# Two-layer hybrid decoder: sums of squares per head by a product with a block matrix of ones, and inverse roots as an exponential of a logarithm

## The chip, the core and the metric

The kernel runs on one core of a Trainium2 chip. A core has five engines with queues of their own: TensorE (PE in the profile; its weight loads stand apart as PEld), VectorE (DVE), ScalarE (ACT), GpSimd (POOL) and SyncE (SP), which here issues most of the DMAs. They wait for one another through semaphores. The metric is the device time of one execution in microseconds (us), taken as the median over runs.

## What is computed

Two layers of a decoder over a prompt of 1024 tokens and a sample group of 8 x 4 = 32 tokens, side by side, so that 1056 columns go through every dense step. Each layer makes all queries, keys and values in one projection, normalises queries and keys per head, rotates a quarter of each head, runs two attention mixers, and ends in an output projection and a gated feed-forward block. The part that the change touches is this one:

```python
def rms_norm(x, g):
    xf = x.astype(jnp.float32)
    y = xf * lax.rsqrt(jnp.mean(xf * xf, axis=-1, keepdims=True) + EPS)
    return (y * g.astype(jnp.float32)).astype(x.dtype)

def mix_inputs(x, g_attn, w_in, qn_a, kn_a, qn_b, kn_b, pos):
    h = rms_norm(x, g_attn)
    proj = jnp.einsum('nld,de->nle', h, w_in)
    qa, ka, va, qb, kb, vb = jnp.split(proj, SPLITS, axis=-1)
    qa = rope_partial(rms_norm(heads(qa, N_HEADS_A), qn_a), pos)
    ka = rope_partial(rms_norm(heads(ka, N_HEADS_A), kn_a), pos)
    qb = rope_partial(rms_norm(heads(qb, N_HEADS_B), qn_b), pos)
    kb = rope_partial(rms_norm(heads(kb, N_KV_B), kn_b), pos)
```

A head has 64 channels; the norm needs, for each token and head, one over the root of the mean of 64 squares.

## The kernel before

Activations lie with channels on the 128 partitions and tokens along the free dimension (1056 = 3 pieces of W = 352). One unit of the projection stage gives 128 channels, that is two heads, for all tokens. A layer has 18 units: unit 0 (keys of the second mixer), unit 1 (its values), and then for each of four pairs p the units u = 2 + 4p (keys), u + 1 (queries of the first mixer), u + 2 (queries of the second) and u + 3 (values of the first mixer, or of the next pair). `project(u, slot, bank, ns)` makes the pieces `ns` of a unit in PSUM banks `bank`, `bank + 1`, `bank + 2`; a piece is 24 products of 352 columns (8 chunks, each as high x high, low x high and high x low parts, line 404), a whole unit 72. Units alternate between banks 0 to 2 and 3 to 5; banks 6 and 7 are for turns.

Of the 18 units of a layer 13 are queries or keys and are normalised (26 in the two layers). For each of them:
- ACT squares the 1056 columns out of PSUM into `t_buf[1]` (`head_squares`, L704; L734 for unit 0).
- DVE multiplies the projection by the gain into `t_buf[0]` (`roped`, L983), shuffles it into `t_buf[2]` (L987), and multiplies by cosines (L989), later by sines (L997), and adds (L999).
- PE sums the squares (`sum_heads`, L1348): nine products, each with 128 (at last 32) tokens of the squares as the stationary operand and the two columns of `blocks` as the moving one. The sums stand with tokens on partitions, in the first 18 columns of the unit's first bank.
- DVE makes means and reciprocals on these few columns (L992, L996, tile `head_means`); ACT takes roots and spreads each over 64 columns (`roots_of_heads`, L711).
- PE turns them back with nine transposes (`spread_heads`, L1358), so that the inverse roots stand on all channels in the unit's three banks, and DVE multiplies (`k_rope` L1005 into `kt_all`, `q_rope` L1010 and L1014 into `xm` and the sample rows, with a factor of -1).

PE's order is written out by hand: `sum_heads` of a unit comes after the first piece of the next unit, `spread_heads` after its second. Between them stand the turns of keys and values (`turn`, L1366 and L1369: nine transposes each), which ACT (`keep_k`, L726 and L729) and DVE (`keep_v`, L1023 and L1026) take out. The values are turned from `stage`, which ACT fills (`stage_v`, L719) once the store of the keys that lay there has left (`k_out`). POOL splits the weights of each unit into high and low parts (L590, L593), beginning when the unit two before has been projected; SP loads them (`w_load`) and stores turned keys (`k_store`) and values in one order. The attention of the layer begins when every unit has been projected and rotated; then come output projection and feed-forward block, most of the layer.

## Time and profile before

| | us |
|---|---|
| median of three runs | 3083.45 (3083.42 to 3084.25) |
| the profiled execution, its own time | 3081.73 |
| its span, first to last instruction | 3080.1 |
| PE busy | 2887.1 (94%) |
| weight loads busy | 2666.2 (87%) |
| DVE busy | 1189.6 (39%) |
| ACT busy | 825.4 (27%) |
| POOL busy | 507.9 (16%) |
| projection stage of the first layer | 78.3 to 325.2 |

Times inside the profile are counted from the first instruction of the span. In a row of the timeline or of the groups, "out<-in" names the tiles by the program's names, then the shapes follow and "x18" is how many records the row merges. PE records overlap, since a product begins before the one ahead has left the array: the start to start distance is the cost of one, the duration isn't. In brackets stands how long the engine was idle before the instruction, and what it waited for. DMA issues stand under the queue of the engine that issues them (SPq, ACTq).

### The profile page before, as it was taken

Reading aid. Unit: us, or ns where it says so; the run is one execution under the profiler, and the core shown is the slowest. Engines: PE = TensorE matmul, PEld = TensorE weight load, DVE = VectorE, ACT = ScalarE, POOL = GpSimd, SP = SyncE. Lnnn points to the kernel's source line nnn. Section 1 sums busy time; section 2 is a strip of 40 time slices with the busy share of each in tenths; the row PEclk is TensorE's granted clock in tenths of the full one; section 3 lists DMA queues with packets and bytes.
Section 4 is the critical chain, followed back from the end, with each engine's and each line's share of the span. In section 5 each row is a group of like instructions: output and inputs, shape, how many; then the busy total and the mean of one; then the engine's idle time right before and its main releaser. Section 6 shows DMA issues by size and latency. Waiting matters only on the chain.

```text
span 3080.1 us, 52475 instructions
## 1 busy us (share of the span) xinstructions
PE 2887.1 (94%) x19546; PEld 2666.2 (87%) x19546; DVE 1189.6 (39%) x2524; ACT 825.4 (27%) x1612; POOL 507.9 (16%) x211
## 2 busy tenths in 40 slices
PE   4999999969899999999969999997889999999998
PEld 4999666569899999999959996665879999999998
DVE  5444555442422222223254445554442222223223
ACT  2111556531211121111031126565221111111110
POOL 1222000012211121112022210000221211122110
PEclk6999999979899999999989999998889999999999
DMA  4121453121455545411021224431245454444111
GB/s 157 43 62 49 117 150 101 51 91 62 166 187 184 179 152 178 151 41 45 9 93 49 55 60 142 128 99 40 91 139 171 152 178 151 151 158 158 41 41 56
DMA packets 182635, 333.36 MB, mean 108 GB/s; under 512 B 30481, under 2 KB 142097, under 8 KB 179665
## 3 DMA queue, kind: packets, MB, share of 16 engines
q1 hardware_dynamic: 171632, 195.20, 20.2%
q0 software_dynamic: 2816, 135.99, 13.3%
q8 instruction: 91, 1.49, 0.2%
q10 hardware_dynamic: 8032, 0.17, 0.2%
q14 instruction: 64, 0.52, 0.1%
HBM read 309.08 MB, written 157.94 MB: 152 GB/s over the span
## 4 chain that ended last, share of the span: by engine, by line
PE 90%; DVE 4%; issue 2%; ACT 2%; DMA 1%; DVEq 0%; ACTq 0%; SPq 0%
PE ps L404 68%; PE ps L1438 4%; PE ps L1452 3%; PE ps L1427 3%; PE ps L1348 2%; PE ps L1501 1%; PE ps L1358 1%; PE ps L1489 1%; PE ps L1470 1%; DVE g_lo L960 1%; DVE t_buf L945 1%; PE ps L1313 1%; DVE hf L945 1%; PE ps L1477 1%; DMA kt_all<-in_x_prompt_dram 1%
## 5 line engine op out<-in xcount | busy, mean ns | idle before, releaser
L404 PE MATMUL ps<-g_hi,f_hi 128*128 128x352 f32 x2496 | 815.6, 327 | 32.7 <-DVE g_lo L960 32.7
L404 PE MATMUL ps<-g_hi,f_lo 128*128 128x352 f32 x2496 | 811.3, 325 | 0.0
L404 PE MATMUL ps<-g_lo,f_hi 128*128 128x352 f32 x2496 | 810.0, 325 | 0.0
L404 PEld LDWEIGHTS ps<-g_hi,f_hi 128*128 128x128 f32 x2496 | 475.1, 190 | 38.2 <-DVE g_lo L960 38.2
L629 POOL TENSOR_TENSOR f_lo<-f_raw,f_hi 128x2048 fp32r<-128x2048 f32 x66 | 303.9, 4618 | 1195.8 <-ACT f_hi L877 1195.8
L404 PEld LDWEIGHTS ps<-g_hi,f_lo 128*128 128x128 f32 x2496 | 475.9, 191 | 0.0
L404 PEld LDWEIGHTS ps<-g_lo,f_hi 128*128 128x128 f32 x2496 | 475.6, 191 | 0.0
L1271 DVE TENSOR_TENSOR silu<-silu,ps 128x352 f32<-128x352 f32 x132 | 68.8, 521 | 820.0 <-ACT silu L899 820.0
L1281 DVE TENSOR_TENSOR xm<-xm,ps 128x352 f32<-128x352 f32 x528 | 271.0, 520 | 199.6 <-PE ps L404 199.6
L404 PE MATMUL ps<-a_hi,f_hi 128*128 128x352 f32 x1056 | 340.6, 323 | 0.0
L404 PE MATMUL ps<-a_hi,f_lo 128*128 128x352 f32 x1056 | 338.4, 320 | 0.0
L404 PE MATMUL ps<-a_lo,f_hi 128*128 128x352 f32 x1056 | 338.2, 320 | 0.0
L404 PE MATMUL ps<-h_hi,w_hi 128*128 128x352 f32 x864 | 288.5, 334 | 14.6 <-DVE h_lo L960 14.6
L404 PE MATMUL ps<-h_lo,w_hi 128*128 128x352 f32 x864 | 279.7, 324 | 0.0
L404 PE MATMUL ps<-h_hi,w_lo 128*128 128x352 f32 x864 | 278.9, 323 | 0.0
L899 ACT ACTIVATE silu<-ps 128x352 f32<-128x352 f32 x132 | 61.3, 465 | 653.4 <-PE ps L404 653.2
L404 PEld LDWEIGHTS ps<-a_hi,f_lo 128*128 128x128 f32 x1056 | 198.4, 188 | 0.0
L404 PEld LDWEIGHTS ps<-a_hi,f_hi 128*128 128x128 f32 x1056 | 198.1, 188 | 0.0
L404 PEld LDWEIGHTS ps<-a_lo,f_hi 128*128 128x128 f32 x1056 | 197.9, 187 | 0.0
L765 ACT ACTIVATE pt<-ps 128x512 f32<-128x512 f32 (+3 forms) x320 | 133.8, 438 | 218.0 <-PE ps L1438 217.3
L404 PEld LDWEIGHTS ps<-h_hi,w_hi 128*128 128x128 f32 x864 | 163.4, 189 | 19.1 <-DVE h_lo L960 17.4
L404 PEld LDWEIGHTS ps<-h_hi,w_lo 128*128 128x128 f32 x864 | 164.1, 190 | 0.0
(166 smaller groups left out, 3360.7 us busy)
## 6 DMA issues: line engine op xcount, KB each, us to landing
out_dram<-in_cache_a_dram POOLq DMA_DIRECT2D x16, 8176.0 KB, 27.2
f_raw<-in_w_gate_up_dram SPq DMA_DIRECT2D x44, 1024.0 KB, 6.3
f_raw<-in_w_down_dram SPq DMA_DIRECT2D x22, 1024.0 KB, 4.9
k_near<-in_cache_a_dram SPq DMA_DIRECT2D x16, 1024.0 KB
v_near<-in_cache_a_dram SPq DMA_DIRECT2D x16, 1024.0 KB
w_raw<-in_w_in_dram SPq DMA_DIRECT2D x28, 512.0 KB, 3.9
k_far<-in_cache_a_dram SPq DMA_DIRECT2D x16, 768.0 KB
v_far<-in_cache_a_dram SPq DMA_DIRECT2D x16, 768.0 KB
```

The lines of the kernel that those rows point to most:

```text
L404: mm = pe.matmul(out, left(a, c), right(b, c), start=(start and c == 0 and k == 0), stop=(stop and c == n - 1 and k == 2))
L629: nc.gpsimd.tensor_tensor(f_lo[j][:], f_raw[j % 2][:], f_hi[j][:].bitcast(F32), ALU.subtract).then_inc(f_split.sem, 1)
L765: nc.scalar.activation(pt[:, g % 4, 0:(b - a) * P], ps[:, 3 + g % 2, 0:(b - a) * P], ACT.Copy).then_inc(pt_ready.sem, 1)
L899: nc.scalar.activation(silu[:, k % 2, :], ps[:, 2 * (k % 2), 0:W], ACT.Silu).then_inc(silued.sem, 1)
L945: nc.vector.tensor_tensor(acc[:, 0:T], acc[:, 0:T], sq[:, 0:T], ALU.add).then_inc(sq_added.sem, 1)
L960: nc.vector.tensor_tensor(lo[:, first + c - 1, :], hf[(c - 1) % 2][:], hi[:, first + c - 1, :].bitcast(F32), ALU.subtract).then_inc(lo_rea ...
L1271: nc.vector.tensor_tensor(silu[:, k % 2, :], silu[:, k % 2, :], ps[:, 2 * (k % 2) + 1, 0:W], ALU.mult).then_inc(gated.sem, 1)
L1281: nc.vector.tensor_tensor(xs, xs, ps[:, 4 + (n * DC + d) % 4, 0:W], ALU.add).then_inc(ffn_added.sem, 1)
L1348: mm = pe.matmul(ps[0:rows_of(t), bank, 2 * t:2 * t + 2], t_buf[1][:, t * P:t * P + rows_of(t)], blocks[:], start=True, stop=True)
L1427: pe.matmul(ps[:, k % 3, 0:w], xm[half, p + (NP if m == "b" else 0), i * P:(i + 1) * P], kt_all[half, 1 + p if m == "a" else 0, first:firs ...
L1438: mm = pe.transpose(ps[:, 3 + g % 2, (c - a) * P:(c - a + 1) * P], probs_of(d, hh)[:, c * P:(c + 1) * P], ident[:])
L1452: mm = pe.matmul(ps[half, 5, 0:P], v_all[:, 1 + p if m == "a" else 0, tiles[c], half], pt[:, g % 4, (c % 4) * P:(c % 4 + 1) * P], start=(c ...
```

## The change

`blocks` grows from two columns to a 128 x 128 matrix with ones in its two diagonal 64 x 64 blocks. `sum_heads` becomes three products per unit, with `blocks` as the stationary operand and 352 columns of squares as the moving one; all three banks of the unit are overwritten with sums that stand on every channel of their head. ACT reads these banks with a logarithm (scale 1/64, bias EPS) into `t_buf[1]`, waits for itself, and takes the exponential of -1/2 times that, on 1056 columns both; a logarithm waits for `head_summed`. `spread_heads`, `head_means`, its DVE steps and `head_spread` are gone, and DVE's last products read `t_buf[1]` instead of PSUM; the sign goes into the first multiplication. Two orders on PE move: the piece 0 of units u, u + 2 and u + 3 is released by the logarithm that read these banks and no longer by the last product of DVE, and the turn of a unit's keys comes after that piece 0 and no longer before it. `head_squares` waits for the last product of the unit before (the `rope` count) where it waited for `head_spread`.

```diff
--- before.py
+++ after.py
@@ -74,7 +74,7 @@
-    c["c_blocks"] = np.kron(np.eye(2), np.ones((HD, 1))).astype(np.float32)
+    c["c_blocks"] = np.kron(np.eye(2), np.ones((HD, HD))).astype(np.float32)
...
@@ -131,7 +131,7 @@
-        blocks = tensor(ctx, "blocks", [P, 2])
+        blocks = tensor(ctx, "blocks", [P, P])
...
@@ -167,7 +167,6 @@
-        head_means = tensor(pairs, "head_means", [P, 2, 2 * (QT + 1)])
...
@@ -257,13 +256,12 @@
-        K_ROPE, Q_ROPE = 10, 12
+        K_ROPE, Q_ROPE = 6, 8
...
-        head_spread = Signal("head_spread", 1 + 3 * NP)
...
@@ -698,20 +696,20 @@
-                def head_squares(unit, bank, n):
+                def head_squares(unit, bank, r):
...
-                    act.wait_ge(head_spread.sem, head_spread.at(l, n))
+                    act.wait_ge(rope.sem, rope.at(l, r))
...
-                def roots_of_heads(n, r):
-
-
-                    act.wait_ge(rope.sem, rope.at(l, r + 7))
-                    for rows, a, b in ((P, 0, QT), (NS, QT, QT + 1)):
-                        nc.scalar.activation(
-                            t_buf[1][0:rows, a * P:b * P].rearrange("p (t d) -> p t d", d=HD),
-                            head_means[0:rows, 1, 2 * a:2 * b].rearrange("p (t o) -> p t o", o=1).broadcast_to(
-                                (rows, 2 * (b - a), HD)), ACT.Sqrt).then_inc(head_root.sem, 1)
+                def roots_of_heads(n, bank):
+
+
+                    act.wait_ge(head_summed.sem, head_summed.at(l, n + 1))
+                    nc.scalar.activation(pieces(t_buf[1][:, 0:T]), banks(bank), ACT.Ln, scale=1.0 / HD,
+                                         bias=eps[:, 0:1]).then_inc(head_root.sem, 1)
+                    act.wait_ge(head_root.sem, head_root.at(l, 2 * n + 1))
+                    nc.scalar.activation(t_buf[1][:, 0:T], t_buf[1][:, 0:T], ACT.Exp, scale=-0.5
+                                         ).then_inc(head_root.sem, 1)
...
                 def stage_v(unit, n):
...
@@ -740,13 +738,13 @@
-                    head_squares(u, 0, h)
-                    roots_of_heads(h, r)
-                    head_squares(u + 1, 3, h + 1)
+                    head_squares(u, 0, r)
+                    roots_of_heads(h, 0)
+                    head_squares(u + 1, 3, r + K_ROPE)
...
-                    roots_of_heads(h + 1, r + K_ROPE)
-                    head_squares(u + 2, 0, h + 2)
-                    roots_of_heads(h + 2, r + K_ROPE + Q_ROPE)
+                    roots_of_heads(h + 1, 3)
+                    head_squares(u + 2, 0, r + K_ROPE + Q_ROPE)
+                    roots_of_heads(h + 2, 0)
...
                 def softmax(d, hh):
@@ -974,47 +972,39 @@
-                def roped(unit, bank, gain, r, root):
+                def roped(unit, bank, gain, sign, r, root):
...
-                    nc.vector.tensor_scalar(pieces(t_buf[0][:]), banks(bank), gains[:, gain:gain + 1], None,
-                                            ALU.mult).then_inc(rope.sem, 1)
+                    nc.vector.tensor_scalar(pieces(t_buf[0][:]), banks(bank), gains[:, gain:gain + 1], sign,
+                                            ALU.mult, ALU.mult).then_inc(rope.sem, 1)
...
-                    dve.wait_ge(head_summed.sem, head_summed.at(l, root + 1))
-                    for rows, a, b in ((P, 0, 2 * QT), (NS, 2 * QT, 2 * QT + 2)):
-                        nc.vector.tensor_scalar(head_means[0:rows, 0, a:b], ps[0:rows, bank, a:b], 1.0 / HD, EPS,
-                                                ALU.mult, ALU.add).then_inc(rope.sem, 1)
+                    nc.vector.tensor_tensor(t_buf[2][:], t_buf[2][:], sin[:], ALU.mult).then_inc(rope.sem, 1)
+                    dve.wait_ge(rope.sem, rope.at(l, r + 4))
+                    nc.vector.tensor_tensor(t_buf[0][:], t_buf[0][:], t_buf[2][:], ALU.add).then_inc(rope.sem, 1)
+                    dve.wait_ge(head_root.sem, head_root.at(l, 2 * root + 2))
...
-                    for rows, a, b in ((P, 0, 2 * QT), (NS, 2 * QT, 2 * QT + 2)):
-                        nc.vector.reciprocal(head_means[0:rows, 1, a:b], head_means[0:rows, 0, a:b]).then_inc(rope.sem, 1)
-                    nc.vector.tensor_tensor(t_buf[2][:], t_buf[2][:], sin[:], ALU.mult).then_inc(rope.sem, 1)
-                    dve.wait_ge(rope.sem, rope.at(l, r + 8))
-                    nc.vector.tensor_tensor(t_buf[0][:], t_buf[0][:], t_buf[2][:], ALU.add).then_inc(rope.sem, 1)
-                    dve.wait_ge(head_spread.sem, head_spread.at(l, root + 1))
-                    dve.wait_ge(rope.sem, rope.at(l, r + 9))
...
                 def k_rope(unit, gain, r, root, kt):
-                    roped(unit, 0, gain, r, root)
-                    nc.vector.tensor_tensor(kt, t_buf[0][:], flat(0), ALU.mult).then_inc(rope.sem, 1)
+                    roped(unit, 0, gain, 1.0, r, root)
+                    nc.vector.tensor_tensor(kt, t_buf[0][:], t_buf[1][:, 0:T], ALU.mult).then_inc(rope.sem, 1)
...
                 def q_rope(unit, bank, gain, r, root, q, rows):
...
-                    roped(unit, bank, gain, r, root)
-                    nc.vector.scalar_tensor_tensor(q, t_buf[0][:, 0:SEQ], -1.0, flat(bank)[:, 0:SEQ],
-                                                   ALU.mult, ALU.mult).then_inc(rope.sem, 1)
+                    roped(unit, bank, gain, -1.0, r, root)
+                    nc.vector.tensor_tensor(q, t_buf[0][:, 0:SEQ], t_buf[1][:, 0:SEQ], ALU.mult).then_inc(rope.sem, 1)
...
-                        nc.vector.scalar_tensor_tensor(rows[half, :, hh * TS:(hh + 1) * TS],
-                                                       t_buf[0][half, SEQ:T].rearrange("p (b t) -> p b t", t=TS), -1.0,
-                                                       flat(bank)[half, SEQ:T].rearrange("p (b t) -> p b t", t=TS),
-                                                       ALU.mult, ALU.mult).then_inc(rope.sem, 1)
+                        nc.vector.tensor_tensor(rows[half, :, hh * TS:(hh + 1) * TS],
+                                                t_buf[0][half, SEQ:T].rearrange("p (b t) -> p b t", t=TS),
+                                                t_buf[1][half, SEQ:T].rearrange("p (b t) -> p b t", t=TS),
+                                                ALU.mult).then_inc(rope.sem, 1)
...
                 def keep_v(n, v, rows):
...
@@ -1344,20 +1334,10 @@
-                    for t in range(QT + 1):
-                        mm = pe.matmul(ps[0:rows_of(t), bank, 2 * t:2 * t + 2], t_buf[1][:, t * P:t * P + rows_of(t)],
-                                       blocks[:], start=True, stop=True)
+                    for c in range(NW):
+                        mm = pe.matmul(ps[:, bank + c, 0:W], blocks[:], t_buf[1][:, c * W:(c + 1) * W],
+                                       start=True, stop=True)
...
-
-                def spread_heads(bank, n):
-
-                    pe.wait_ge(head_root.sem, head_root.at(l, 2 * n + 2))
-                    pe.sem_inc(waits_alone, 1)
-                    for t in range(QT + 1):
-                        w = rows_of(t)
-                        mm = pe.transpose(ps[:, bank + t // 4, (t % 4) * P:(t % 4) * P + w],
-                                          t_buf[1][0:w, t * P:(t + 1) * P], ident[0:w, 0:w])
-                    mm.then_inc(head_spread.sem, 1)
...
                 def turn(src, rest, done):
...
@@ -1379,15 +1359,15 @@
                 mm.then_inc(projected.sem, 1)
                 project(1, 1, 3, (0,))
                 sum_heads(0, 0, 0)
-                project(1, 1, 3, (1,))
-                spread_heads(0, 0)
-                project(1, 1, 3, (2,))
+                project(1, 1, 3, (1, 2))
                 for p in range(NP):
                     u, r, h = 2 + 4 * p, K_ROPE + ROPE_P * p, 1 + 3 * p
-                    pe.wait_ge(rope.sem, rope.at(l, r))
+                    pe.wait_ge(head_root.sem, head_root.at(l, 2 * h - 1))
+                    project(u, 0, 0, (0,))
                     if p == 0:
+                        pe.wait_ge(rope.sem, rope.at(l, r))
                         turn(kt_all[:, 0, :], 2, k_turned)
-                    project(u, 0, 0, (0, 1))
+                    project(u, 0, 0, (1,))
                     pe.wait_ge(v_staged.sem, v_staged.at(l, p + 1))
                     pe.wait_ge(k_kept.sem, k_kept.at(l, 3 * p + 3))
                     turn(stage, 5, v_turned)
@@ -1395,23 +1375,20 @@
                     project(u + 1, 1, 3, (0,))
                     sum_heads(0, h, r)
                     project(u + 1, 1, 3, (1,))
-                    spread_heads(0, h)
                     pe.wait_ge(v_kept.sem, v_kept.at(l, 3 * p + 3))
                     project(u + 1, 1, 3, (2,))
+                    pe.wait_ge(head_root.sem, head_root.at(l, 2 * h + 1))
+                    project(u + 2, 0, 0, (0,))
                     pe.wait_ge(rope.sem, rope.at(l, r + K_ROPE))
                     turn(kt_all[:, 1 + p, :], 2, k_turned)
-                    project(u + 2, 0, 0, (0,))
                     sum_heads(3, h + 1, r + K_ROPE)
                     project(u + 2, 0, 0, (1,))
-                    spread_heads(3, h + 1)
                     pe.wait_ge(k_kept.sem, k_kept.at(l, 3 * p + 6))
                     project(u + 2, 0, 0, (2,))
-                    pe.wait_ge(rope.sem, rope.at(l, r + K_ROPE + Q_ROPE))
+                    pe.wait_ge(head_root.sem, head_root.at(l, 2 * h + 3))
                     project(u + 3, 1, 3, (0,))
                     sum_heads(0, h + 2, r + K_ROPE + Q_ROPE)
-                    project(u + 3, 1, 3, (1,))
-                    spread_heads(0, h + 2)
-                    project(u + 3, 1, 3, (2,))
+                    project(u + 3, 1, 3, (1, 2))
                 pe.wait_ge(rope.sem, rope.at(l, K_ROPE + NP * ROPE_P))
...
                 def score(d, c):
```

## Rows read from the trace of the kernel before

**Rows 1.** The page's busy times, granted clock in tenths, and the chain that ended last
```profile
PE 2887.1 (94%) x19546; PEld 2666.2 (87%) x19546; DVE 1189.6 (39%) x2524; ACT 825.4 (27%) x1612; POOL 507.9 (16%) x211
...
PEclk6999999979899999999989999998889999999999
...
PE 90%; DVE 4%; issue 2%; ACT 2%; DMA 1%; DVEq 0%; ACTq 0%; SPq 0%
```

**Rows 2.** Busy time of each engine by stretch; then granted clock, DMA share, GB/s
```profile
78.30:106.50 28.20, 28.20 (x191) 27.88 (x190) 9.69 (x15) 4.59 (x7) 6.89 (x4) 1.00 0.16 41
106.50:164.50 58.00, 58.00 (x390) 57.15 (x389) 26.34 (x40) 9.09 (x13) 13.76 (x8) 1.00 0.20 55
...
280.00:325.20 45.20, 45.20 (x307) 44.37 (x306) 24.85 (x37) 8.04 (x12) 6.88 (x4) 1.00 0.09 26
```

**Rows 3.** Groups of PE products by shape: sums (L1348) and spreads (L1358)
```profile
L1348 PE MATMUL ps<-blocks,t_buf 128*128 128x2 f32 x416 | 47.9, 246 | 0.0
...
L1358 PE MATMUL ps<-ident,t_buf 128*128 128x128 f32 x208 | 26.9, 272 | 0.0
...
L1348 PE MATMUL ps<-blocks,t_buf 128*32 128x2 f32 x52 | 5.8, 182 | 0.0
```

**Rows 4.** Timeline of PE around one sum and one spread (start, length)
```profile
110.07 0.32 PE L404 MATMUL ps<-h_lo,w_hi 128*128 128x352 f32 x1
...
112.42 0.32 PE L404 MATMUL ps<-h_hi,w_lo 128*128 128x352 f32 x1
...
115.94 0.33 PE L404 MATMUL ps<-h_lo,w_hi 128*128 128x352 f32 x1
...
117.50 0.32 PE L404 MATMUL ps<-h_hi,w_lo 128*128 128x352 f32 x1
```

**Rows 5.** Timeline of ACT; each of these starts when a unit is projected
```profile
106.67 1.05 ACT L704 ACTIVATE t_buf<-ps 128x1056 f32<-128x1056 f32 x1 [9.03 <-PE ps L404]
...
121.48 1.05 ACT L704 ACTIVATE t_buf<-ps 128x1056 f32<-128x1056 f32 x1 [7.39 <-PE ps L404]
...
137.22 1.06 ACT L704 ACTIVATE t_buf<-ps 128x1056 f32<-128x1056 f32 x1 [7.36 <-PE ps L404]
...
152.05 1.05 ACT L719 ACTIVATE stage<-ps 128x1056 f32<-128x1056 f32 x1 [7.40 <-PE ps L404]
164.61 1.06 ACT L704 ACTIVATE t_buf<-ps 128x1056 f32<-128x1056 f32 x1 [11.51 <-PE ps L404]
```

**Rows 6.** Timeline of PE: sample scores, full-precision products on four groups of 32 columns
```profile
359.35 1.06 PE L1489 MATMUL ps<-kt_s,q_rows_a 128*32 128x512 f32 x8
...
359.80 0.61 PE L1489 MATMUL ps<-kt_s,q_rows_a 128*32 128x512 f32 x4
```

**Rows 7.** Timeline of DVE in unit 3 of the first layer
```profile
122.57 1.32 DVE L983 TENSOR_SCALAR t_buf<-ps,gains 128x1056 f32<-128x1056 f32 x1 [3.88 <-ACT t_buf L704]
...
133.20 1.22 DVE L1010 SCALAR_TENSOR_TENSOR xm<-t_buf,ps 128x1024 f32<-128x1024 f32 x1 [2.18 <-PE ps L1358]
```

**Rows 8.** Timeline of ACT: loads of its function tables
```profile
33.60 1.28 ACT L677 ACT_TABLE_LOAD   x1 [33.60 <-DVEq L964]
...
47.79 1.28 ACT L684 ACT_TABLE_LOAD   x1
...
326.72 1.28 ACT L755 ACT_TABLE_LOAD   x1
```

**Rows 9.** Timeline around the first turn of keys: PE, ACT, ACT's DMA queue
```profile
93.81 0.27 PE L1369 MATMUL ps<-ident,kt_all 128*32 128x128 f32 x1
...
94.97 0.39 ACTq L738 DMA_DIRECT2D out_dram<-stage  x1
96.58 1.06 ACT L719 ACTIVATE stage<-ps 128x1056 f32<-128x1056 f32 x1 [1.78 <-DMA out_dram<-stage]
```

**Rows 10.** DMA issues: line, count, KB each, median us from issue to landing
```profile
w_raw<-in_w_in_dram SPq DMA_DIRECT2D x28, 512.0 KB, 3.9
```

**Rows 11.** Who waited for whom, 75 to 326 us: total, times, longest
```profile
POOL w_hi L590 <- PE ps L404: 187.4, 16, 25.1
```

## The prediction

> **What bounds the kernel now.** I began with the page's busy times and the chain that ended last: PE is busy 94% of the span and carries 90% of the chain, the other engines 4% or less of it [rows 1]. Then came the granted clock by slices, to see which stretches run at 2.4 GHz, and the busy times by stretch. In the projection stage, the only one that the change touches, PE is busy without a break at the full clock: 28.20 us of 28.20, 58.00 of 58.00, 45.20 of 45.20, while DVE is at 45% and ACT at 16% [rows 2]. In this stretch a microsecond that PE doesn't have to work is a microsecond less, and work on DVE or ACT costs nothing until PE waits for it. Outside it nothing is changed, save for one table load and one constant.
>
> **What PE loses.** There are 468 sum records and 234 of spreads (208 of them shown), that is 18 and 9 for each of 26 normalised units; a sum has nine products, so in this precision a product is two records [rows 3]. Their durations overlap and can't be added. I take the distance of the ordinary products on either side instead: from 110.07 to 112.42 is 2.35 us, of which two ordinary slots of 0.16 would be there anyway, so a sum costs 2.03; from 115.94 to 117.50 is 1.56, so a spread costs 1.24 [rows 4]. Together 3.27 us a unit. The slot of 0.16 is (115.94 - 112.42) / 22. A second way: ACT's first instruction after each unit shows the units' lengths, 14.81, 15.74, 14.83 and 12.56 us [rows 5]; 12.56 is 72 products and one turn, 15.74 the same with a sum and a spread, so these cost 3.18; the two without a turn have 72 x 0.16 = 11.52 of products and give 3.29 and 3.31. So 3.18 to 3.31, and I take 3.27.
>
> **What PE gets.** Three products of 352 columns with a full 128 x 128 stationary operand, in the same precision as the old sums, so six records. The trace has no untiled one of this kind. Nearest are the sample's scores: eight records of 512 columns on four groups of 32 array columns, begun at 359.35; the second round of four begins at 359.80 [rows 6]. If the four of a round run side by side, a record of 512 columns takes 0.43 to 0.45 us, two cycles of 2.4 GHz per column (0.427), and one of 352 columns 0.293 to 0.31. If they ran one after another they would take 0.11 us each, under the 0.16 that 352 columns of the cheap kind need, which I can't believe. So six records at 0.293 are 1.76 us. On the way back to ordinary products the sum of before loses 0.11 (0.27 from the first ordinary product to the second, where 0.16 is usual); I add it: 1.87 us. The bounds are 1.80 (the loss mostly hidden, since weights can load under a product of 0.29) and 1.97 (0.31 a record).
>
> **The difference.** 3.27 - 1.87 = 1.40 us a unit, times 26 is 36.4 us; between bounds, (3.18 - 1.97) x 26 = 31.5 and (3.31 - 1.80) x 26 = 39.3.
>
> **Does the cover hold?** Each removed wait has a successor. I follow one sum through the new order, with rows for each step (an ACT instruction on 1056 columns 1.06 [rows 5], a first multiplication on DVE 1.32, a last one 1.22 [rows 7]).
> - Squares to sum: unit projected, ACT 0.15 later for 1.06, DVE 1.32 (it waits for the squares, to keep two engines off one bank). Ready 2.6 us after the unit's end; PE comes after one piece, 24 x 0.16 = 3.8 us. Slack 1.2, unchanged.
> - Sum to the piece that overwrites its banks: only the logarithm has to be done, about 1.2 us after the sum; two pieces, 7.7 us, lie between. Slack 6.
> - Sum to the last multiplication and from it to the next squares, the new wait of `head_squares`: logarithm 1.1, exponential 1.1, multiplication 1.2 and 0.4 for the sample rows, some 4.2 with hand-overs, against 7.7 of pieces. Slack 3.5. The tightest case is unit u + 2, where ACT must first take the turned keys out: the turn ends at 3.8 + 1.0 us into the unit, ACT is done some 1.0 later, at 5.8, and the sum ends at 6.7. Still the sum comes last. Queued behind the waiting logarithm on ACT are only the exponential and the next squares, and no one needs these before the unit ends.
> - The keys' turn comes a piece later. Behind it hang `k_store` and the next `w_load` on SP's queue: issued about 6.5 us into a unit of 14.4, landing 3.9 later [rows 10], where POOL wants the weights at the unit's end. POOL always waits for PE today, 187.4 us in all over 16 units, and its 3.6 us of splitting have the following unit of 13.4 as cover [rows 11]. Slack 4 and more.
> - Only at the first pair is it tight. The turn of unit 0's keys moves behind the first piece, so one piece (3.8 us) and no longer two covers what hangs on it: turn over at 94.08, keys taken out, stored by ACT's own DMA (issue at 94.97), `stage_v` from 96.58 to 97.64 [rows 9]. That is 3.6 us, slack 0.2. A store that is slower by half a microsecond stalls PE by 0.3; over two layers I allow 0 to 2 us and take 0.2.
>
> DVE loses its small steps on `head_means` and reads its factor from SBUF and no longer from PSUM; as it isn't waited for, nothing comes of it, and I put it at zero both ways. The larger `blocks` is 63 KB more in front of the input tiles' loads in the first 16 us; at the 157 GB/s of the page's first slice this is up to 0.4 us, which I take.
>
> **Function tables.** The trace shows the old order with one table for the whole stage: a load of 1.28 us before the first square, another before the first root, none for squares, roots and copies until the softmax, and one there [rows 8]. The new one needs at least one load more for the logarithm after the roots of the layer's first norm, and saves the one before the softmax, where PE was waiting for DVE. The second row also says how loads are placed: the table loaded for the squares didn't hold the root, though one that holds both exists (no load follows when squares come back). So the choice isn't made with the next function in view, and logarithm and exponential may come from different tables: two loads in each of 26 units, 26 x 2 x 1.28 = 67 us on ACT. The one before the logarithm runs ahead of its wait, as the one at 47.79 did, and only that before the exponential lies between sum and multiplication: 4.2 becomes 5.5 us, against 7.7. In unit u + 2 the first load ends at 7.1 and the product at about 12.7, of 14.4. Cost on PE's path zero in either case. The Trainium skill, "ScalarE: Activation LUTs", section "Table sets: the hidden batching unit", speaks against this change: calls should be batched by set, and a root stage in one set is turned into one that leaves it; it also says that one set holds both logarithm and exponential. By its 2.7 us for every switch, drain included, two switches in each of 26 units would be an estimated 140 us on ACT, still not on PE. This trace agrees on the load itself (1.28) and can't show which set is chosen.
>
> **Sum.** Against the profiled execution, 3081.73: -36.4 + 0.2 + 0.4 = -35.8, so 3045.9. The median stands 1.7 above that execution, so 3083.45 - 35.8 = 3047.6; I say 3047.5.
>
> **Rivals.**
> 1. *The new products are dearer (slower than before).* If an untiled product of this kind took twice what the tiled rows say, 0.587 a record, the sum would cost 3.52 + 0.11 = 3.63 us, 0.36 more than today's sum and spread: 9.4 us more in all, 3093. It turns from a gain to a loss at (3.27 - 0.11) / 6 = 0.53 us a record. Against it: the second round at 0.45 us for 512 columns. For it: no row of the untiled shape. Chance 4%.
> 2. *They are cheaper.* At one cycle per column, 0.16 a record as ordinary products, the sum costs 0.95 + 0.11 = 1.06 and the gain is 57.5: 3026. Against it the same row, 0.45 where 0.21 would do. Chance 3%.
> 3. *A new wait eats the gain.* If the alternating table load came onto PE's path in each normalised unit (1.28 x 26 = 33 us), 2.5 us would be left: 3081, no change that can be told. It needs the chain behind the sum to be longer by over 2 us than worked out, for instance a logarithm that costs more than a square. With both loads on the path, it would be 30 us slower than before. Chance 3% for both, 2 and 1. A part of it, waits of 0.2 to 0.6 us in each unit, gives 3058 to 3068: chance 5%.
> 4. *The change doesn't do what it says*, PE still waiting where the spreads stood: within case 3.
>
> **How the numbers follow.** Forecast, with its bounds: 85%. The range takes the bounds 31.5 and 39.3 of the difference, the 0 to 2 us of the first pair, 0 to 0.4 of the constant and 1 us of scatter: 3042 to 3055; with a little of case 3 on the slow side and the softmax's saved load on the other, 3040 to 3057. Left out are rivals 1 to 3, 15%, and some of the forecast's own tail. A measurement of this kernel can tell about 0.2%, 6 us. Faster by more: forecast, rival 2 and the part of 3, 93%. Within: 2%. Slower: 4% from rival 1, 1% from rival 3: 5%.
>
> **What would show it right or wrong.** Right: six records in each sum, 0.29 apart; no spread; units of 13.4, 14.4, 13.4 and 12.6 us where there were 14.8, 15.7, 14.8 and 12.6; PE busy throughout the stage, which ends about 18 us earlier in the first layer; ACT from 16% to some 20% of it, or over 30% with alternating tables. Wrong: records 0.16 or 0.5 us apart, or rows of PE that wait for ACT's logarithm, for `stage` or for DVE's last product.

## The result, and the profile after

| | before | changed |
|---|---|---|
| median, us | 3083.43 (3077.93 to 3084.25) | 3042.05 (3039.55 to 3044.45) |
| ratio | | 0.9869, 95% interval 0.9856 to 0.9882 |
| span of the profiled execution | 3080.1 | 3038.0 |

The change takes 41.4 us off, 1.3%. Forecast were 3047.5 us and a range of 3040 to 3057. The time fell as forecast and for the reason given, and the gain is 5.4 us larger.

The place of the gain is read best from ACT: its first instruction after each unit marks the unit's end. Timeline of ACT in the changed kernel, the units that [rows 5] shows of before, and the last one of the stage:

```profile
106.23 1.05 ACT L702 ACTIVATE t_buf<-ps 128x1056 f32<-128x1056 f32 x1 [5.27 <-PE ps L402]
107.30 1.28 ACT L708 ACT_TABLE_LOAD   x1
111.74 1.15 ACT L708 ACTIVATE t_buf<-ps,eps 128x1056 f32<-128x1056 f32 x1 [3.15 <-PE ps L1338]
112.90 1.28 ACT L711 ACT_TABLE_LOAD   x1
114.20 1.09 ACT L711 ACTIVATE t_buf<-t_buf 128x1056 f32<-128x1056 f32 x1
119.45 1.05 ACT L702 ACTIVATE t_buf<-ps 128x1056 f32<-128x1056 f32 x1 [4.17 <-PE ps L402]
...
133.75 1.06 ACT L702 ACTIVATE t_buf<-ps 128x1056 f32<-128x1056 f32 x1 [4.04 <-PE ps L402]
...
147.07 1.05 ACT L717 ACTIVATE stage<-ps 128x1056 f32<-128x1056 f32 x1 [4.24 <-PE ps L402]
159.54 1.05 ACT L702 ACTIVATE t_buf<-ps 128x1056 f32<-128x1056 f32 x1 [11.41 <-PE ps L402]
...
306.57 1.05 ACT L717 ACTIVATE stage<-ps 128x1056 f32<-128x1056 f32 x1 [4.17 <-PE ps L402]
```

Units of 14.81, 15.74, 14.83 and 12.56 us have become 13.22, 14.30, 13.32 and 12.47. From the first unit's end to the last one's (I call this the stage below) the first layer takes 228.46 us where it took 247.25, the second 228.08 where it took 247.17: 37.9 us in all. The stage is the measure of everything that follows, since it repeats within some 0.4 us from trace to trace of one kernel, while whole times scatter by several.

Timeline of PE around one sum (before: [rows 4]), and the group of sums:

```profile
109.61 0.32 PE L402 MATMUL ps<-h_lo,w_hi 128*128 128x352 f32 x1
109.77 1.94 PE L1338 MATMUL ps<-t_buf,blocks 128*128 128x352 f32 x6
111.27 0.59 PE L402 MATMUL ps<-h_hi,w_hi 128*128 128x352 f32 x1
111.71 0.32 PE L402 MATMUL ps<-h_hi,w_lo 128*128 128x352 f32 x1
```
```profile
L1338 PE MATMUL ps<-t_buf,blocks 128*128 128x352 f32 x156 | 50.4, 459 | 0.0
```

Six records, 156 in 26 sums as forecast. From 109.61 to 111.71 is 2.10; two ordinary slots of 0.16 off, a sum costs 1.78 us.

PE's busy time in the two projection stages, from the view by stretch; the first row of each fence is the projection, the second the attention of the first layer. Before:

```profile
78.40:325.65 247.25, 247.25 (x1658) 243.32 (x1658) 113.58 (x172) 39.92 (x59) 55.07 (x32) 1.00 0.18 48
325.65:632.10 306.45, 284.13 (x2537) 186.32 (x2536) 158.10 (x590) 180.08 (x515) 0.00 (x0) 0.97 0.37 106
```

Changed:

```profile
78.11:306.57 228.46, 227.30 (x1385) 218.28 (x1385) 107.28 (x120) 86.40 (x84) 55.14 (x32) 1.00 0.19 52
306.57:609.60 303.03, 279.00 (x2537) 184.27 (x2536) 158.21 (x590) 178.32 (x514) 0.00 (x0) 0.98 0.38 107
```

ACT's busy time in the stage doubles, from 39.92 to 86.40 us, and PE is still busy but for 1.16 us. That one wait is new; it stands in the waits of PE:

```profile
PE ps L1346 <- ACT stage L717: 2.3, 2, 1.2
```

### The profile page after: what moved, and what is told of

Read it like the earlier page. It is cut to its first block, busy times and chain, and to the rows that moved or that the text cites. A ratio compares the mean times of both kernels' runs of the same rounds, so it can differ in the third digit from the quotient of the medians.

```text
span 3038.0 us, 51313 instructions
## 1 busy us (share of the span) xinstructions
PE 2839.4 (93%) x19000; PEld 2612.0 (86%) x19000; DVE 1175.8 (39%) x2420; ACT 915.5 (30%) x1662; POOL 507.5 (17%) x211
## 4 chain that ended last, share of the span: by engine, by line
PE 89%; DVE 5%; issue 3%; ACT 2%; DMA 1%; DVEq 0%; ACTq 0%; SPq 0%
PE ps L402 68%; PE ps L1415 4%; PE ps L1429 3%; PE ps L1404 3%; PE ps L1338 2%; PE ps L1478 1%; DVE g_lo L958 1%; PE ps L1466 1%; PE ps L1447 1%; DVE t_buf L943 1%; PE ps L1303 1%; DVE hf L953 1%; PE ps L1454 1%; DVE hf L943 1%; DMA kt_all<-in_x_prompt_dram 1%
```

## Experiments

All stages are given for first and second layer. The kernel before has 247.2 and 247.2, the changed one 228.5 and 228.1.

**The changed kernel again, for what lies outside the stage.**

> The changed kernel once more beside the kernel before. The projection stages of the two traces differ by 18.8 and 19.1 us, 37.9 in all, the medians by 41.4. If the rest is the attention's clock falling one way or another in single executions, the difference of medians comes out at 37 to 42 again and the two stages at 228.5 and 228.1 us within 0.3. If the change itself gave the rest, it is 41 or more, and the attention of both layers is 3 us shorter than 306.4 and 307.6.

Measured: 3042.31 us against 3080.57 of before beside it, 38.3 less, ratio 0.9871 (0.9854 to 0.9887); stages 228.6 and 228.3, both as expected. The first result's 41.4 and this 38.3 are one figure within their intervals, and the stages account for 37.9 of it. The attentions of this trace (from the stage's end to ACT's first instruction of the next norm) took 310.1 and 305.9 us, those of the first 303.0 and 306.4, those of before 306.4 and 307.6. Two traces of the same kernel differ by more here than the two kernels do, so the rest can't be told from scatter of the attention, whose work is the same in all. The changed kernel's attention isn't 3 us shorter.

**The load before the softmax, taken off the path in the kernel before.** [rows 8] showed a table load of 1.28 us at 326.72, which the change does away with. In the first 20 us of the attention the granted clock (the number after the POOL column) was 0.83 before and 1.00 in the changed kernel, a tempting cause. Views by stretch, before and then changed:

```profile
325.70:345.70 20.00, 17.73 (x109) 10.11 (x107) 10.17 (x41) 13.53 (x44) 0.00 (x0) 0.83 0.98 290
```
```profile
306.60:326.60 20.00, 17.09 (x131) 10.64 (x130) 11.96 (x49) 13.24 (x45) 0.00 (x0) 1.00 0.97 286
```

```diff
+                    if n == 3 * NP:
+                        nc.scalar.activation(early[:, 0:1], eps[:, 0:1], ACT.Exp)
```

> The kernel before, with one exponential of one column after the last root of each layer, so that the softmax's table is loaded while PE is still projecting. Theory A (scatter): the same as before, 3081 to 3085. Theory B (the load at the start of the attention costs PE a wait and with it clock): 3 to 5 us under the kernel before, about 3079, and granted clock 1.00 in the first 20 us of the attention.

The load now stands at 318.18, under PE's work:

```profile
318.18 1.28 ACT L717 ACT_TABLE_LOAD   x1
319.48 0.20 ACT L717 ACTIVATE early<-eps 128x1 f32<-128x1 f32 x1
325.53 1.05 ACT L722 ACTIVATE stage<-ps 128x1056 f32<-128x1056 f32 x1 [5.85 <-PE ps L405]
```

Time: 3082.56 us against 3080.18, ratio 1.0007 (0.9997 to 1.0017). No gain. In this trace the first 20 us of the first attention did run at 1.00, those of the second at 0.83, and both attentions were long (309.2 and 308.5). The changed kernel's second trace speaks the same way: no load stands before its softmax either, and the first 20 us of its first attention ran at 0.74, of its second at 0.91. So neither the load nor the change sets the clock of this stretch. Theory A holds, and the saved load is worth nothing that can be measured.

**A root and a reciprocal instead of logarithm and exponential**, with PE's new work kept.

```diff
-                    nc.scalar.activation(pieces(t_buf[1][:, 0:T]), banks(bank), ACT.Ln, scale=1.0 / HD,
-                                         bias=eps[:, 0:1]).then_inc(head_root.sem, 1)
-                    act.wait_ge(head_root.sem, head_root.at(l, 2 * n + 1))
-                    nc.scalar.activation(t_buf[1][:, 0:T], t_buf[1][:, 0:T], ACT.Exp, scale=-0.5
-                                         ).then_inc(head_root.sem, 1)
+                    nc.scalar.activation(pieces(t_buf[1][:, 0:T]), banks(bank), ACT.Sqrt, scale=1.0 / HD,
+                                         bias=eps[:, 0:1]).then_inc(head_root.sem, 2)
...
                     dve.wait_ge(head_root.sem, head_root.at(l, 2 * root + 2))
+                    nc.vector.reciprocal(t_buf[1][:, 0:T], t_buf[1][:, 0:T]).then_inc(rope.sem, 1)
```

> The changed kernel with a root on ACT and a reciprocal on DVE, both on all 1056 columns, in place of logarithm and exponential. PE's order and work are those of the changed kernel. The 52 table loads inside the projection stage go, and the load before the softmax is back. Theory A (the stage is PE's work alone, loads and chain are covered, and the 4 us beyond the stage are scatter of the attention's clock): the same as the changed kernel within 2 us, 3040 to 3044. Theory B (the missing load before the softmax is what lets the attention start without a slower clock): 3 to 5 us slower than the changed kernel, 3045 to 3047, with the granted clock below 1.00 in the first 20 us of the attention. Rival C (the loads cost PE something): faster than the changed kernel by over 2 us.

Measured: 3108.13 us, ratio 1.009 (1.0073 to 1.0106), slower than before. All three expectations missed, because I had taken the reciprocal to cost what DVE's other steps on 1056 columns cost. Timeline of DVE in unit u + 2:

```profile
130.79 6.75 DVE L989 RECIPROCAL t_buf<-t_buf 128x1056 f32<-128x1056 f32 x1
137.57 2.84 DVE L999 TENSOR_TENSOR xm<-t_buf 128x1024 f32<-128x1024 f32 x1
140.34 0.40 DVE L1002 TENSOR_TENSOR q_rows_a<-t_buf 64x32 f32<-64x32 f32 x2
```

6.75 us where a product takes 1.26. The last product ends late, the next unit's first multiplication with it, and PE stands:

```profile
PE ps L1336 <- DVE t_buf L978: 30.5, 16, 4.0
```

The stages are 254.5 and 254.9, 26 and 27 us over the changed kernel. In each, PE is idle for 17 us; most of the rest goes with the granted clock, 0.97 and 0.96 where the changed kernel has 1.00. So the part of the change on ACT does matter, though not for PE's work: on all channels the inverse root has to be made somewhere in 7.6 us, and DVE's reciprocal doesn't fit. This run can't tell the cost of the table loads; the next one does.

**Two idle copies in the chain.** On ACT between logarithm and exponential (`idle` is read by no one):

```diff
                     act.wait_ge(head_root.sem, head_root.at(l, 2 * n + 1))
+                    for j in range(2):
+                        act.wait_ge(idled.sem, idled.at(l, 2 * n + j))
+                        nc.scalar.activation(idle[:], cos[:], ACT.Copy).then_inc(idled.sem, 1)
```

> The changed kernel with two idle copies of 1056 columns on ACT between logarithm and exponential, 2.3 us more in the chain from each sum to the last multiplication. By the rows of the changed kernel the tightest unit (u + 2) has 2.0 us to the next squares and 1.2 more to the sum. Theory: hidden, under 2 us in all, 3042 to 3044. Rival (the chain is already late somewhere): 10 us and more.

Measured: 3043.91 us, ratio 0.9883 (0.9868 to 0.9898); stages 228.4 and 228.5. Nothing of the added time reaches PE, though the two copies take 2.21 us and a table load 1.28. Had the load before the exponential been on the path, these copies would be too.

**Five idle copies.**

> The same with five idle copies, some 6 us more in the chain. Theory: the cover of 3.2 us (units u + 2) and 4.0 us (units u + 1) is used up: waits of 2.8 and 2.0 us in each of eight pairs and of some 4 us at the end of each stage, 35 to 50 us in all, 3077 to 3092. Rival (the cover is larger than I read): under 10 us.

Measured: 3131.91 us, ratio 1.017 (1.0154 to 1.0186): 90 us over the changed kernel, about twice what I expected. The cover ends between the two copies (2.2 us) and the five (5.6 us), which agrees with the 3.2 and 4.0 that I had read; the price beyond it is higher. Timelines of DVE and POOL in units u + 1 and u + 2:

```profile
121.68 3.31 DVE L1001 TENSOR_TENSOR kt_all<-t_buf 128x1056 f32<-128x1056 f32 x1 [7.20 <-ACT t_buf L716]
...
138.91 3.29 DVE L1006 TENSOR_TENSOR xm<-t_buf 128x1024 f32<-128x1024 f32 x1 [6.21 <-ACT t_buf L716]
```
```profile
120.25 1.04 POOL L590 CAST w_hi<-w_raw 128x1024 fp32r<-128x1024 f32 x1 [9.64 <-PE ps L404]
121.47 2.41 POOL L593 TENSOR_TENSOR w_lo<-w_raw,w_hi 128x1024 fp32r<-128x1024 f32 x1 [0.18 <-POOL w_hi L590]
...
138.71 2.40 POOL L593 TENSOR_TENSOR w_lo<-w_raw,w_hi 128x1024 fp32r<-128x1024 f32 x1 [0.18 <-POOL w_hi L590]
```

DVE's last product takes 3.3 us, not 1.26. Pushed past the unit's end, it falls together with POOL's splitting of the next weights and gets 2 us longer still. That makes waits of up to 4.0 us for the first multiplication, and behind such a wait the clock is lower: the sum at 145.00, after 4.03 us of waiting, takes 2.87 us for its six records where the one at 109.77 of the changed kernel takes 1.94. PE's waits, and the granted clock (the number after the POOL column) in the stretches 124 to 142 and 142 to 156 us:

```profile
PE ps L1343 <- DVE t_buf L986: 37.6, 16, 4.0
...
PE ps L1351 <- DVE kt_all L1001: 13.0, 10, 1.3
```
```profile
124.00:142.00 18.00, 14.69 (x87) 13.49 (x87) 10.44 (x8) 12.40 (x13) 3.44 (x2) 1.00 0.22 60
142.00:156.00 14.00, 11.00 (x53) 9.93 (x54) 6.83 (x9) 10.18 (x9) 0.00 (x0) 0.88 0.13 39
```

Stages: 266.0 and 263.7, 73 us in all over the changed kernel. PE is idle in them for 26.7 and 27.0 us, where the changed kernel has 1.2; most of the other 10 to 12 us a layer goes with the granted clock (0.96 and 0.97). Behind each stage PE waits 3.3 us more for the last multiplication. The two stretches outside the stages are 11 us longer in this trace than in the first one of the changed kernel, those waits included.

**The price of the new sum: its products done twice.**

```diff
-                    for c in range(NW):
+                    for c in (*range(NW), *range(NW)):
```

> The changed kernel with each sum's three products done twice over. It prices a sum by itself. Theory (six records of 0.293 us, nothing hidden): 26 x 1.76 = 45.8 us more than the changed kernel, 3088. If a good part of the sum's cost were the change to and from the ordinary products, it would be less than 40.

Measured: 3092.65 us, ratio 1.004 (1.0025 to 1.0055). Stages 252.1 and 252.2, 23.9 us more a layer and 47.7 in all; over 13 sums a layer that is 1.84 us for six records, 0.306 each. So no good part of the cost is in the change to and from the ordinary products. The record is nearer to the 0.31 of my upper bound, the scaled 0.45 of [rows 6], than to the 0.293 that I took; the way out costs nothing, since six records in place cost 1.78 and not 1.95.

**The price of the old sum: its products done twice in the kernel before.**

```diff
-                    for t in range(QT + 1):
+                    for t in (*range(QT + 1), *range(QT + 1)):
```

> The kernel before with each sum's nine narrow products done twice. It prices the sum that the change removes: 2.03 us by the rows around one sum, so 26.4 us a layer and 53 in all, each stage 273.6 us. If the price of a sum were mostly the way in and out of it, it would be under 20 us a layer.

Measured: 3185.42 us, ratio 1.0343 (1.0325 to 1.0361), 105 us more, where 53 were expected. The stages are 294.8 and 296.1 us, 47.5 and 48.9 over the kernel before, where 26.4 were expected. A unit without a turn grew from 14.8 to 18.3 us. Timeline of PE behind one doubled sum:

```profile
117.14 0.41 PE L1348 MATMUL ps<-blocks,t_buf 128*128 128x2 f32 x3
117.48 0.54 PE L404 MATMUL ps<-h_hi,w_hi 128*128 128x352 f32 x1
117.82 0.50 PE L404 MATMUL ps<-h_hi,w_lo 128*128 128x352 f32 x1
118.11 0.50 PE L404 MATMUL ps<-h_lo,w_hi 128*128 128x352 f32 x1
118.40 0.50 PE L404 MATMUL ps<-h_hi,w_hi 128*128 128x352 f32 x1
```

The doubled sum itself takes 4.03 us for 2.00, so 2.03 was the right price for one. But then some 12 ordinary products come 0.29 us apart and not 0.16, which is 352 columns at 1.2 GHz; that is 1.5 us more than usual behind each sum, the whole excess of the unit. The granted clock of the stretch is 0.91, where the kernel before has 1.00 in [rows 2]:

```profile
110.00:128.30 18.30, 18.30 (x120) 17.99 (x119) 8.13 (x11) 2.28 (x3) 3.44 (x2) 0.91 0.10 30
```

PE was never idle: what it did before the clock fell was 36 records that load their weights, 32 of them 128 columns, and push two columns through. The single sum of before, 18 such records, kept the clock. Both theories spoke only of the sum's own price, and it is the one expected; the clock wasn't in either.

**The first turn of keys ahead again.** PE waits for `stage` 1.2 us in each layer of the changed kernel. In its trace (timelines of ACT and of SP's queue):

```profile
96.97 0.39 ACTq L736 DMA_DIRECT2D out_dram<-stage  x1
99.92 1.05 ACT L717 ACTIVATE stage<-ps 128x1056 f32<-128x1056 f32 x1 [3.11 <-DMA out_dram<-stage]
```
```profile
95.49 1.00 SPq L462 DMA_DIRECT2D w_raw<-in_w_in_dram  x2
```

```diff
-                    pe.wait_ge(head_root.sem, head_root.at(l, 2 * h - 1))
-                    project(u, 0, 0, (0,))
                     if p == 0:
                         pe.wait_ge(rope.sem, rope.at(l, r))
                         turn(kt_all[:, 0, :], 2, k_turned)
-                    project(u, 0, 0, (1,))
+                    pe.wait_ge(head_root.sem, head_root.at(l, 2 * h - 1))
+                    project(u, 0, 0, (0, 1))
```

> The changed kernel with the first pair's turn of keys back ahead of the piece 0, so that two pieces cover keeping, store and staging. Theory: the two waits of PE for stage (2.3 us in all) go and nothing else becomes late: 2 to 3 us under the changed kernel, about 3039.5. Rival: the turn now waits for the last multiplication of unit 0 (logarithm, load, exponential, multiplication: 5.5 us after the sum, 7.6 us of pieces over it), or the wait only moves: within 1 us of the changed kernel.

Measured: 3037.76 us, ratio 0.9862 (0.9845 to 0.9878), against 3080.18 beside it. The time alone can't tell it from the changed kernel, the stages can: 226.9 and 227.1, 1.5 and 1.0 us less, and the wait for `stage` is gone from PE's list. No wait took its place.

**Squares in the short format.** Written by ACT in the format of the projection's high parts, into a tile of their own; the squares are rounded to it.

```diff
+        squares = tensor(pairs, "squares", [P, T], F32R)
...
-                    nc.scalar.activation(pieces(t_buf[1][:, 0:T]), banks(bank), ACT.Square).then_inc(head_sq.sem, 1)
+                    nc.scalar.activation(pieces(squares[:]), banks(bank), ACT.Square).then_inc(head_sq.sem, 1)
...
-                        mm = pe.matmul(ps[:, bank + c, 0:W], blocks[:], t_buf[1][:, c * W:(c + 1) * W],
+                        mm = pe.matmul(ps[:, bank + c, 0:W], blocks_r[:], squares[:, c * W:(c + 1) * W],
```

> The changed kernel with the squares written in the short format (the same as the high parts of the projection's operands), so that a product of a sum is one record and not two; the squares are rounded to it. Theory (a record costs two cycles per column in full precision and one in the short format): sums cost 3 x 0.16 = 0.48 plus up to 0.2, in place of 1.78; 1.1 to 1.3 us less in each of 26 units, 29 to 34 us in all: 3008 to 3013. Rival (the cost of a sum is mostly switching and loading weights): under 15 us in all.

Measured: 3009.7 us, ratio 0.9771 (0.9755 to 0.9788). A sum is three records and takes one ordinary slot for each:

```profile
108.80 0.32 PE L404 MATMUL ps<-h_lo,w_hi 128*128 128x352 f32 x1
108.96 0.64 PE L1341 MATMUL ps<-squares,blocks_r 128*128 128x352 f32 x3
109.44 0.32 PE L404 MATMUL ps<-h_hi,w_hi 128*128 128x352 f32 x1
109.60 0.32 PE L404 MATMUL ps<-h_hi,w_lo 128*128 128x352 f32 x1
```

0.48 us, with no loss on the way in or out. Units of 13.22 become 11.92, the stages 212.0 and 212.0. The rival is out.

**Both together.**

> Squares in the short format and the first turn of keys ahead, together. Both theories hold side by side: 31 to 36 us under the changed kernel, 3006 to 3011. If shorter units take away cover (3.8 us of pieces over 2.6 us of squares and first multiplication is unchanged, but the turn of keys and the weights' loads come closer), PE waits appear and it is 3012 or more.

Measured: 3008.91 us (3002.74 to 3010.27), ratio 0.9769 (0.9755 to 0.9782); stages 210.5 and 210.7. It is the fastest of all here, 2.3% under the kernel before, though its time can't be told from that of the short squares alone. No new wait appears.

## Why the prediction came out as it did

**PE bounds the stage, and what it need not do is gained.** Right: 37.9 us of the gain lie in the two stages, and the trace of the changed kernel shows PE busy there except for 1.2 us a layer.

**The removed work, 3.27 us, was priced right, but the units shrank by a little more.** The doubled old sum bears out 2.03 for a sum. The short squares seem to say more: a unit of 11.92 us less a sum of 0.48 is 11.44 for 72 products, and 14.80 - 11.44 is 3.36 us, outside my bounds of 3.18 to 3.31. But this takes the ordinary products to be alike in both kernels, and they aren't: their slot, averaged over the stages from the start times, is 0.1600 us in both layers of the kernel before and 0.1593 and 0.1590 in the changed one. Over the 1296 ordinary products of a layer this is 0.9 to 1.3 us. Single stretches have slots from 0.159 to 0.161 in both kernels, and what moves them no run here shows.

**The added work, 1.87 us, was priced slightly high.** It is 1.78, below my lower bound of 1.80. The record costs 0.30 to 0.306 (near its upper bound), and the 0.11 for the way back to ordinary products doesn't arise: two errors that nearly cancel, which is luck. I had taken the bare two cycles per column (0.293) for the new record while the 0.16 of the ordinary one was measured, and that one too stands 0.013 above its bare cycle per column (0.147). Per unit the sums and spreads make 3.27 - 1.78 = 1.49 in place of 1.40, so 26 x 1.49 = 38.7 us and not 36.4. The rows show somewhat more, 14.81 to 13.22 where no turn stands and 1.54 on average over the first layer's twelve normalised units of the pairs; the difference is the closer ordinary products.

**The cover.** Right in all the chains of the pairs: no wait for the logarithm or for DVE stands in the stages. In unit u + 2, begun at 119.30, the first table load ends at 126.15 (6.9 us in, 7.1 forecast), and DVE's last product with its sample rows at 131.37 (12.1 in, 12.7 forecast). Two copies more fit in, five don't.

**The first pair.** Rows of PE that wait for `stage` were among my signs of being wrong, and this one came. The mechanism was named, its size was off: 2.3 us of waits for 0.2 taken, 0 to 2 allowed. I had 3.6 us from the turn's end to the staging, from [rows 9]. In the changed kernel the store is issued at 96.97, 1.5 us behind the loads of 512 KB of weights on SP's queue, and takes 1.3 us longer than in [rows 9] (2.95 from issue to staging, 1.61 there). With five idle copies it is issued 3.0 us behind the same loads and takes 1.62 again. The traces agree in both layers: 1.6 where the store goes out before the loads or 3.0 us behind them, 2.8 to 3.0 where 1.5 behind, 3.5 and 3.6 in the run with root and reciprocal, where 0.7 behind. No run moved the loads alone, but what this DMA takes goes with what it falls together with, and I had moved it without asking that.

**The terms together.** 38.7 us of sums and spreads, less the 2.5 that the run with the turn ahead got back, is 36.2. The two stages gained 37.9; the remaining 1.7 is of the size of the closer ordinary products (0.9 to 1.3 a layer).

**The constant, 0.4.** Nothing of it shows: the first unit ends at 78.40 before and 78.11 after. Over all traces this moment scatters from 77.7 to 78.8, so 0.4 can't be told.

**Function tables.** The poorer of the two cases came true. Groups of ACT in the changed kernel:

```profile
L708 ACT ACT_TABLE_LOAD x26 | 33.4, 1283 | 0.5
L711 ACT ACT_TABLE_LOAD x26 | 33.4, 1283 | 0.5
```

52 loads, 66.8 us of ACT's time, at no cost to PE, as forecast (67 us, zero). The reading of [rows 8], that a load is placed without the next function in view, was enough for that. The Trainium skill, "ScalarE: Activation LUTs", section "Table sets: the hidden batching unit", gives one load for a logarithm and an exponential together; this trace disagrees, with a load before each. Nor does it show the 2.7 us of a switch: the logarithm ends at 112.89, the load starts at 112.90 and the exponential at 114.20, 1.30 later.

**Beyond the stage.** Nothing changed there, as forecast. The median's gain of 41.4 in the first comparison and 38.3 in the second stand around the stages' 37.9. Attentions of equal work took from 303.0 to 310.1 us in the traces of the changed kernel alone. That my 36 was 5 us short of the first median is 2 us of prices, slots and waits in the stages and 3.5 us outside them, where scatter is larger than that.

**The range.** My terms don't reach its fast side: 3083.45 - 39.3 - 1 of scatter is 3043.2, where I wrote 3042, and only the allowance for the softmax's saved load, which proved worth nothing, brought it to 3040. The first median, 3042.05, lies in that strip. That it fell inside is in part luck; the gain of the stages, 37.9, and that of the second comparison, 38.3, lie inside the bounds of the difference.

**The rivals.** Dearer records: out, 0.306 against the 0.53 needed. Cheaper: out for this format; it holds for the short one, 0.16 a record. A wait that eats the gain: not here, but the run with five copies shows it is real once the chain grows by 5.6 us (by 2.2 it isn't), and it then costs more than the lateness itself. Its smaller part was added up wrongly: waits of 0.2 to 0.6 us in each of 26 units are 5 to 16 us, which gives 3053 to 3063 and not 3058 to 3068.

## What to carry to other kernels

Where one engine is busy without a break, count its instructions by their distance, not their duration, in the stretch concerned, and keep three digits of the ordinary slot: it is multiplied by everything, and between two kernels it can differ by half a per cent. A narrow product isn't cheap: with two moving columns a record took 0.11 us, with 352 in the same precision 0.30. Put the constant matrix in the stationary place and the wide data in the moving one, and the turn back is saved too. When a DMA is moved, list what it will meet in its new place, and when a chain moves, what its engine shares with others there.

## What the runs showed of the hardware that I had not expected

- TensorE's clock can fall while it is busy: behind 36 records of two columns each (4.03 us without idle time) it was at 1.2 GHz, and some 12 products took 0.29 us and not 0.16; behind 18 such records it was at 2.4.
- DVE's reciprocal on 128 x 1056 takes 6.75 us, 5.4 times a product of the same size (1.26).
- A DVE product of two SBUF tiles takes 3.3 us in place of 1.26 when it begins while POOL subtracts two SBUF tiles. In the run with five copies the product begun at 121.68 ended 1.1 us after POOL's subtraction (123.88), the one begun at 138.91 as much after the next (141.11), and POOL kept its 2.4: the one that came second did most of its work after the first had ended. In the run with root and reciprocal it was seen the other way: POOL's 2.40 became 3.22 when it ran against DVE, whose product of 1.26 us had begun at 121.91 (timeline of POOL):

```profile
122.19 3.22 POOL L591 TENSOR_TENSOR w_lo<-w_raw,w_hi 128x1024 fp32r<-128x1024 f32 x1 [0.18 <-POOL w_hi L588]
```

The change turned one operand of these products from PSUM to SBUF, which I had put at zero. Where they don't meet POOL's splits it is: 1.22 us before and after for the products into `xm`.
